# Hybrid Hyena/attention step on one core: another order of first loads and steps, modulation in four column groups, odd stream blocks by ScalarE, filters one by one between projections

## The reference, cut to what matters

```
shift, scale, gate = jnp.split(mod, 3, axis=-1)      # mod = silu(c) @ w_mod + b_mod
h = x * (1 + scale) + shift
proj = h @ p['w_in'][l]                              # 66 column blocks of 128
filt = hyena_filters(n, ...)                         # sin MLP on positions, @ w3, times a decay
y_hy = hyena(hy_in, conv_w, conv_b, filt, skip)      # 2 orders of long convolution
... differential attention, MLA, gates, merge, w_out, LayerNorm

def hyena_filters(...):
    hid = jnp.sin(sf[0] * (feats @ w1 + b1))
    hid = jnp.sin(sf[1] * (hid @ w2 + b2))
    h = hid @ w3
    h = h * jnp.exp(-t_lin[:, None] * jnp.exp(log_decay))
```

## Time and profile before

| | before |
|---|---|
| device time, median of 3 runs | 2047.17 us (2043.9 to 2050.02) |
| the profiled execution | 2044.92 us, of which the profile's span is 2043.1 us |
| PE busy | 1902.6 us, 93% of the span |
| DVE busy | 1112.3 us, 54% |
| ACT busy | 640.1 us, 31% |
| POOL busy | 495.1 us, 24% |
| granted TensorE clock, mean | 0.979 |

### The profile page before, as it was taken

The page is one execution under the profiler, slowest core; times in us unless marked ns, Lnnn a source line. Parts: engine busy times, 40 slices in busy tenths (PEclk is TensorE's granted clock), DMA queues, the critical chain, the costliest instruction groups (busy, mean ns, idle before and its releaser), DMA issues.

```text
span 2043.1 us, 28064 instructions
## 1 busy us (share of the span) xinstructions
PE 1902.6 (93%) x11444; PEld 1630.7 (80%) x11444; DVE 1112.3 (54%) x1571; ACT 640.1 (31%) x1132; POOL 495.1 (24%) x228
## 2 busy tenths in 40 slices
PE   6799899999999999999968999999999999999995
PEld 4579599887786777899965876998788777779995
DVE  3458568355343443377776775745453434444744
ACT  2231321244333444322233222123442344442221
POOL 0210104222231111276320010332222301115551
PEclk9899999999999999999978999999999999999998
DMA  9011012111220101354620111221113100114431
GB/s 343 22 36 48 31 63 73 55 45 47 78 83 21 35 32 31 109 177 139 248 83 31 42 32 31 83 68 47 42 52 109 42 23 28 32 47 132 173 109 52
DMA packets 50159, 151.83 MB, mean 74 GB/s; under 512 B 11051, under 2 KB 12587, under 8 KB 48753
## 3 DMA queue, kind: packets, MB, share of 16 engines
q1 hardware_dynamic: 46432, 135.89, 19.8%
q10 hardware_dynamic: 3600, 14.16, 2.0%
HBM read 143.43 MB, written 6.59 MB: 73 GB/s over the span
## 4 chain that ended last, share of the span: by engine, by line
PE 81%; DVE 9%; ACT 4%; issue 3%; SPq 1%; DMA 1%; POOL 1%; ACTq 0%; DVEq 0%; POOLq 0%
PE PS L776 19%; PE PS L781 18%; PE PS L777 18%; PE PS L831 6%; PE PS L967 3%; PE PS L819 2%; PE PS L1085 2%; PE PS L866 2%; PE PS L869 2%; PE PS L1018 2%; PE PS L848 2%; DVE MG L1620 1%; ACT work L1136 1%; ACT Wh L1136 1%; PE PS L1074 1%
## 5 line engine op out<-in xcount | busy, mean ns | idle before, releaser
L1780 POOL TENSOR_TENSOR Wl<-W,Wh 128x1024 fp32r<-128x1024 f32 (+1 forms) x176 | 401.2, 2282 | 1370.5 <-ACT Wh L1136 1328.4
L776 PE MATMUL PS<-Hh,Wh 128*128 128x320 f32 x2048 | 615.8, 315 | 24.6 <-DVE work L1538 10.9
L777 PE MATMUL PS<-Hl,Wh 128*128 128x320 f32 x2048 | 606.4, 311 | 0.0
L776 PEld LDWEIGHTS PS<-Hh,Wh 128*128 128x128 f32 x2048 | 387.9, 189 | 49.8 <-issue 34.7
L777 PEld LDWEIGHTS PS<-Hl,Wh 128*128 128x128 f32 x2048 | 388.0, 189 | 1.4 <-issue 1.2
L781 PE MATMUL PS<-Hh,Wl 128*128 128x320 f32 x2048 | 321.4, 309 | 0.9 <-POOL Wl L1780 0.9
L781 PEld LDWEIGHTS PS<-Hh,Wl 128*128 128x128 f32 x2048 | 305.5, 188 | 1.4 <-POOL Wl L1780 1.4
L1136 ACT ACTIVATE work<-PS 128x640 f32<-128x640 f32 (+10 forms) x322 | 180.8, 575 | 351.4 <-PE PS L831 96.8
L1400 DVE TENSOR_REDUCE st<-PS 128x1 f32<-128x640 f32 (+1 forms) x160 | 114.9, 718 | 281.1 <-PE PS L848 176.2
L1136 ACT ACTIVATE Wh<-W 128x1024 fp32r<-128x1024 f32 x196 | 185.2, 951 | 54.4 <-PE PS L781 28.7
L1248 ACT ACTIVATE th<-PS 128x640 f32<-128x640 f32 x64 | 45.1, 705 | 358.3 <-PE PS L781 358.3
(11 more groups left out here) (194 smaller groups left out, 2545.4 us busy)
## 6 DMA issues: line engine op xcount, KB each, us to landing
W<-in_w_in SPq DMA_DIRECT2D x132, 512.0 KB, 3.5
W<-in_w_branch SPq DMA_DIRECT2D x48, 256.0 KB, 2.6
work<-in_w_mod_rows ACTq DMA_DIRECT2D x23, 512.0 KB, 3.8
pmod_w<-in_w_mod SPq DMA_DIRECT2D x8, 1024.0 KB, 17.2
W<-in_w_out SPq DMA_DIRECT2D x16, 512.0 KB, 5.6
late_modulation_w<-in_w_mod_rows SPq DMA_DIRECT2D x9, 512.0 KB, 7.5
work<-in_x_sample SPq DMA_DIRECT2D x2, 2048.0 KB
x_mid<-work SPq DMA_DIRECT2D x1, 2560.0 KB, 8.4
```

The source lines that it names most:

```text
L776: pe.matmul(out, Wh[:, b, kk, :], xh[:, kk, t], start=kk == 0, stop=False)
L777: pe.matmul(out, Wh[:, b, kk, :], xl[:, kk, t], start=False, stop=False)
L1780: return pool.tensor_tensor(out, in_, high.bitcast(f32), ALU.subtract)
```

## The change

- `pmrow` has four steps in place of eight. Each takes four weight tiles; the conditioning vectors stand in a stationary operand padded with zeros to 32 columns (`cpad`), and the four tiles' results go to PSUM partitions 0, 32, 64 and 96, in the array's four column groups. One transpose of 128 x 128 follows in each of four `pmod` steps.
- First loads: constants, small tables, `feats`, `w3`, log decays, then the eight modulation tiles, weight tile 0, x, weight tile 1, the forward tables; the inverse tables and rope come at `conv` 2. The one semaphore of the Hyena tables becomes three.
- Steps of layer 0: `fdft` 0 and 1 move from ahead of `ht` 0 to after `two` 4 and `conv` 1.
- `ht` c with odd c: ScalarE does the modulation (Identity with scale and bias, from PSUM) as well as the rounding. VectorE does all eight `Hl`; GpSimd none.
- The decay buffer is given back after VectorE's second instruction of a filter (`decay_used`), not its fourth. The Exp of the log decays and the first decay of a layer move to step `lam`.
- Steps of layer 1: `filt` 0 after `two` 2, `filt` 1 after `two` 4, `filt` 2 after `two` 7, `filt` 3 ahead of `conv` 2, `filt` 4 ahead of `conv` 3. While `ht` and `two` alternate, the inner steps take two PSUM slots in turn.

```diff
+def start_steps(ahead, inside):
+    s = [("ht", c) for c in range(4)] + ahead + [("two", 0)]
+    for c in range(4, KD):
+        s += [("ht", c), ("two", c - 3)] + inside.get(c - 3, [])
+    return s + [("two", kk) for kk in range(5, KD)]
 def layer_steps(l):
     if l == 0:
-        p = [("pmod", g) for g in range(KD)]
+        p = [("pmod", g) for g in range(4)]
         f = [("ffn", 0), ("ffn", 1)] + [("filt", t) for t in range(NT)] + [("fdft", i) for i in range(5)]
-        rows = [("pmrow", g) for g in range(KD)]
-        s = [("lam", 0)] + rows[:1] + f[:1] + rows[1:3] + p[:2] + f[1:2] + rows[3:5] + p[2:4] + f[2:3]
-        s += rows[5:6] + p[4:5] + f[3:4] + rows[6:7] + p[5:6] + f[4:5] + rows[7:] + p[6:7] + f[5:6] + p[7:] + f[6:9]
-        s += START
-        s += [("conv", 0), ("conv", 1), ("fdft", 2), ("conv", 2), ("conv", 3), ("fdft", 3), ("fdft", 4)]
+        rows = [("pmrow", g) for g in range(4)]
+        s = [("lam", 0)] + f[:1] + rows[:1] + f[1:2] + rows[1:2] + p[:1] + rows[2:3] + p[1:2] + f[2:4] + rows[3:] + p[2:3]
+        s += f[4:5] + p[3:] + f[5:7] + start_steps([], {4: f[7:8]})
+        s += [("conv", 0), ("conv", 1), ("fdft", 1), ("conv", 2), ("fdft", 2), ("conv", 3), ("fdft", 3), ("fdft", 4)]
     else:
         f = [("filt", t) for t in range(NT)]
-        s = [("lam", 0)] + START
-        s += [("conv", 0), ("conv", 1)] + f[:3] + [("conv", 2)] + f[3:] + [("conv", 3)]
+        s = [("lam", 0)] + start_steps([], {2: f[:1], 4: f[1:2]})
+        s += f[2:3] + [("conv", 0), ("conv", 1)] + f[3:4] + [("conv", 2)] + f[4:] + [("conv", 3)]
         s += [("fdft", i) for i in range(5)]
...
@@ slot_table
+                if rest:
+                    s = rest[0]
+                    rest.reverse()
+                else:
+                    s = at % SLOTS
+                    at += 1
...
+            if (kind, i) == ("two", 0):
+                rest = [at % SLOTS, (at + 1) % SLOTS]
+            elif (kind, i) == ("two", KD - 1):
+                at += 2
+                rest = None
...
@@ SyncE
                 if g >= NP:
-                    sp.wait_ge(*filled(0, "pmrow", g - NP))
+                    sp.wait_ge(*filled(0, "pmrow", (g - NP) // 2))
...
-            first_modulation(0)
...
-            for part in range(4):
+            for part in range(2):
                 layer_tables(0, part)
-            for g in range(1 + len(FIRST), NP):
+            for g in range(KD):
                 first_modulation(g)
+            weight(0)
             load_x(0)
-            for g in range(NP, KD):
-                first_modulation(g)
-            sp.dma_start(rope_m[:], A["rope_m"]).then_inc(rope_here, 16)
+            weight(1)
+            layer_tables(0, 2)
...
+                    if (kind, i) == ("conv", 2) and l == 0:
+                        layer_tables(0, 3)
+                        sp.dma_start(rope_m[:], A["rope_m"]).then_inc(rope_here, 16)
...
@@ TensorE
-                pe.wait_ge(*after("h_odd" if kk % 2 else "h_even", l, kk // 2 + 1))
+                pe.wait_ge(*after("h_lo", l, kk + 1))
...
+                        for g in (2 * i, 2 * i + 1):
+                            pe.wait_ge(pmod_here[g % NP], 16 * (g // NP + 1))
+                        for k in range(KD):
+                            for j in range(4):
+                                last = pe.matmul(ps[32 * j:32 * j + 32, 0:128], cpad[:, k, :],
+                                                 pmod_w[:, (2 * i + j // 2) % NP, j % 2, k, :], start=k == 0, stop=k == KD - 1)
...
@@ ScalarE
                         act.activation(lamc[:, 4:6], lamc[:, 4:6], ACT.Exp).then_inc(sems["lam_exp"], 1)
+                        act.wait_ge(filter_here, 16 * N_FILTER * (l + 1))
+                        link(act.activation(expld, expld, ACT.Exp))
+                        act.activation(decay, expld[:, :, 0, :], ACT.Exp, scale=negt[:, 0:1]).then_inc(sems["decay_ready"], 1)
                     elif kind == "ht":
-                        act.wait_ge(*after("h_f32", l, i + 1))
+                        if i % 2:
+                            act.wait_ge(*filled(l, kind, i))
...
+                            h = th[:, 1]
+                            act.activation(h[:, 0:LAT], ps[:, 0:LAT], ACT.Identity, scale=s[:, 0:1], bias=b[:, 0:1])
+                            act.activation(h[:, LAT:NTOK], ps[:, LAT:NTOK], ACT.Identity, scale=s[:, 1:2], bias=b[:, 1:2])\
+                               .then_inc(sems["h_act"], 1)
+                            act.wait_ge(*after("h_act", l, i // 2 + 1))
+                        else:
+                            act.wait_ge(*after("h_f32", l, i // 2 + 1))
                         copy(Hh[:, i, :], th[:, i % 2]).then_inc(sems["h_hi"], 1)
...
                         if i:
-                            act.wait_ge(*after("fab_ready", l, i))
...
+                            act.wait_ge(*after("decay_used", l, i))
+                            act.activation(decay, expld[:, :, o, :], ACT.Exp, scale=negt[:, t:t + 1]).then_inc(sems["decay_ready"], 1)
@@ VectorE
+                        for c in [i - 1] * (i > 0) + [i] * (i == KD - 1):
+                            dve.wait_ge(*after("h_hi", l, c + 1))
+                            TT(Hl[:, c, :], th[:, c % 2], Hh[:, c, :].bitcast(f32), ALU.subtract).then_inc(sems["h_lo"], 1)
+                            dve.wait_ge(*own("h_lo"))
...
                         TT(oddb[:, 0], ps[:, 0:HY], decay[:, 0], ALU.mult)
-                        link(STT(oddb[:, 1], ps[:, 512:1024], hmask[:, t:t + 1], decay[:, 1], ALU.mult, ALU.mult))
+                        STT(oddb[:, 1], ps[:, 512:1024], hmask[:, t:t + 1], decay[:, 1], ALU.mult, ALU.mult)\
+                            .then_inc(sems["decay_used"], 1)
+                        dve.wait_ge(*own("decay_used"))
@@ GpSimd
-                    if kind == "ht" and i % 2 == 0:
-                        pool.wait_ge(*after("h_hi", l, i + 1))
-                        minus(Hl[:, i, :], th[:, 0], Hh[:, i, :]).then_inc(sems["h_even"], 1)
```

More of the change, by code:

```diff
@@ L225 @@
 JOBS = {
-    "pmod": lambda i: [("ss_ready", 2 * i + 2)],
+    "pmod": lambda i: [("ss_ready", 4 * i + 4)],
     "nmod": lambda i: [],
@@ L293, in slot_table @@
     for l in range(DEPTH):
+        rest = None
         for kind, i in STEPS[l]:
             for j, (name, count) in enumerate(JOBS[kind](i)):
-                late = kind == "ht" and i >= 4
-                s = (at + i % 2) % SLOTS if late else at % SLOTS
+                if rest:
[4 more added lines that the diff above has]
+                    at += 1
                 table[l, kind, i, j] = (s, uses[s], last[s])
@@ L413, in build @@
         Wh = sb("Wh", [128, 2, KD, 128], f32r)
+        Wl_at = at[0]
         Wl = sb("Wl", [128, 2, KD, 128], f32r)
+        cpad = sb("cpad", [128, KD, 32], over=Wl_at)
         MG = sb("MG", [128, KD * NTOK])
@@ L462, in area @@
                                 **{c: d for c, d in zip(names, dims)})
-        pmrow = area(work, 12816, 4, 256)[0:2]
+        pmrow = area(work, 12816, 4, 128)
         ln_gc, ln_bc = vec(vecs, "ln_g"), vec(vecs, "ln_b")
@@ L670, in layer_tables @@
                         continue
-                    if n:
-                        sp.dma_start(dst, src).then_inc(hy_here, 16)
-                    else:
-                        sp.dma_start(dst, src).then_inc(feats_here, 16)
-                    if l == 0 and n in FIRST:
-                        first_modulation(1 + FIRST.index(n))
+                    sp.dma_start(dst, src).then_inc(HERE[part], 16)
             def norm_rows(l):
@@ L878, in _ @@
                         ps = slot(l, kind, i)
-                        pe.wait_ge(pmod_here[i % NP], 16 * (i // NP + 1))
-                        for m in range(2):
-                            for k in range(KD):
-                                last = pe.matmul(ps[0:2, 128 * m:128 * m + 128], ccol[:, k, :],
-                                                 pmod_w[:, i % NP, m, k, :], start=k == 0, stop=k == KD - 1)
+                        for g in (2 * i, 2 * i + 1):
[4 more added lines that the diff above has]
+                                                 pmod_w[:, (2 * i + j // 2) % NP, j % 2, k, :], start=k == 0, stop=k == KD - 1)
                         last.then_inc(full_of(l, kind, i), 1)
@@ L888, in _ @@
                         pe.wait_ge(*after("row_ready", 0, i + 1))
-                        for m in range(2):
-                            last = transpose(ps[:, 2 * m:2 * m + 2], pmrow[:, i % 4, 128 * m:128 * m + 128], 2)
-                        last.then_inc(full_of(l, kind, i), 1)
+                        transpose(ps[:, 0:128], pmrow[:, i]).then_inc(full_of(l, kind, i), 1)
                     elif kind == "ht":
@@ L1175, in _ @@
                         act.wait_ge(*filled(l, kind, i))
-                        if i >= 4:
-                            act.wait_ge(*filled(l, "pmod", i - 4))
```

(13 more changed lines are left out.)

64 lines of the change are left out of this document (30 added, 34 removed).

## The result

| | before | after |
|---|---|---|
| median of the runs (4 each) | 2047.25 us (2043.9 to 2050.02) | 2020.54 us (2018.5 to 2021.73) |
| the profiled execution | 2044.92, span 2043.1 | 2021.73, span 2019.9 |
| granted TensorE clock, mean | 0.979 | 0.981 |

The account below looks back on a forecast made before the run. TensorE is busy 93%, so time is won only where it waits or runs at half clock, as in chains between engines at the start. 23.4 + 4.9 + 2.8 + 2.7 = 33.8 us less gives 2012 us, range 2004 to 2020.

Parts of the forecast that it names:

- the order-1 filters: Both layers: decays come 1.3 earlier, so the last filter ends 2.8 us sooner in layer 0, 2.7 in layer 1.
- `two` 0 at 53.0: Start of layer 0: the first projection starts at 53.0 us, not 83.5, 30.5 less.
- Tiles 0 and 1 "are there at 19": Loads of layer 0: the first two modulation tiles have landed at 19 us, with some 2 us of transfer lost.
- The rival of late loads: Start of layer 0: loads land late, slack 7 us for x, 3 for weight tile 1; 2016 to 2018, chance 0.11.
- "2.5 us" for every `pmrow`: Layer 0 modulation: a step of 64 matmuls takes 2.5 us, with 1.8 and 7.3 as ends.
- The two `Wl`: Start of layer 0: they follow the last decay (46.4), take 4.66 us on GpSimd and end at 52.2.
- the 0.9 for `Hl`: Start of layer 0: `Hl` 0 (0.83 on VectorE) meets the second `Wl`, so `two` 0 starts at 53.0, behind 52.2.
- Groups without overlap: Rival, `pmrow` of layer 0: column groups don't overlap, a step takes 7.3 us; 2019 us in all, chance 0.10.
- First stage slower than before: Rival, start of layer 0: no overlap and half clock, 14.6 us a `pmrow`; 2059 us in all, chance 0.03.
- VectorE isn't the bound: Rival, starts of both layers: VectorE's queue drains faster, `two` 0 starts near 50; 2005 us, chance 0.11.
- the likeliest case: Whole kernel: the forecast itself, 2012 us (2006 to 2017 by the ends of its terms), chance 0.62.

Follow-up runs that it names:

- l_tiles_first: Changed kernel with the first two modulation tiles asked for ahead of the tables and filter weights; 2015.59 us.
- r_same: The changed kernel run and profiled again, unaltered; 2020.55 us.
- y_all: Changed kernel with two modulation tiles loaded first, VectorE making `Wl` 0 and 1 of layer 0, and the decays' Exp ahead of `lam`'s; median 2010.17 us.
- w_vector: Changed kernel with `Wl` 0 and 1 of layer 0 made by VectorE, not GpSimd; 2016.82 us.
- f_decay_late: Changed kernel with the decay buffer given back after a filter's fourth instruction, as before the change; 2027.92 us.

## Why the prediction went as it did

**What held.** The change is faster, and by the mechanism named: with the long chain at the start shortened, `fdft` 0 and 1 behind it cost 7.0 (7.1 forecast), `Hh` 0 of layer 1 starts 3.1 behind the first Exp (3.4), `fdft` 0 there 48.5 and 47.3 behind the first transpose (49), the order-1 filters give 2.7 and 2.6 (2.8 and 2.7), and the collision passes to the short convolution as said. A `pmrow` takes 1.96 us at full clock, between the ends of 1.8 and 7.3; I had taken 2.5. By the 62 ns that the Trainium skill gives for the issue of a matmul when hardware decode is off (TensorE: Matmul & The Clock Gate, the section "Wait — 56ns, not 53.3ns?") it would have been an estimated 4.0. The trace shows 31 ns for each, so that floor doesn't bind here.

**What failed: `two` 0 at 53.0.** It came at 56.6 and 59.2, and four of its steps were wrong. By the means of the pairs the start of layer 0 got 24.6 us shorter, not 30.5, and that is most of the miss.

*Tiles 0 and 1 "are there at 19".* They came at 21.5. The step let the engines run full from 10.5 on; the table by stretch has 304 GB/s up to 15, which makes 2.2 MB by then, not 2.5 (0.8 us). The other 1.6 is sharing, by this sum: at 412 GB/s, 4.8 MB are in by 21.4, 0.7 more than stands up to tile 1, so tiles asked for later took a part. `l_tiles_first` shows that closing the gap, most of which the step had booked as a loss, brings 1.1 to 3.7 us at `two` 0.

*Slack for late loads.* The rival of late loads was given 7 us of slack for x and 3 for weight tile 1. The path doesn't go through x. It goes through the tiles of `pmrow` 2, since `filt` 0 stands behind that step and VectorE's chain of five filters begins there. They were forecast for 29 and came at 31.8 and at 33.0 (in `r_same`, where TensorE waited 3.9 for them). From there on nothing had slack: `filt` 0 was at 34.2 and 36.7, not 32.8, and the 2.6 between the two executions is the 2.6 between their `two` 0.

*"2.5 us" for every `pmrow`.* At full clock it is 1.96, but not every step had the full clock. In `r_same` `pmrow` 2 starts behind a wait of 3.9, and the granted clock is 0.50 while it runs. The timeline, and the table by stretch (length, busy PE with its count, PEclk, DMA share, GB/s):

```profile
32.98 3.55 PE L894 MATMUL PS<-pmod_w,cpad 128*32 128x128 f32 x64 [3.94 <-DMA pmod_w<-in_w_mod]
```

```profile
33.50:36.00 2.50, 2.50 (x55) 0.50 1.02 408
```

So 64 of these matmuls take some 3.6 us at 1.2 GHz and 1.96 at 2.4. Of the 2.6 between the two executions, 1.2 is the tiles of `pmrow` 2 and the rest this clock; in the first profile TensorE had waited only 0.52 there. The 3.64 of `pmrow` 0 is the same size. The column reads 1.00 there, as it does from 20 to 25 us in every profile but that of `y_all`. But the four matmuls of `ffn` 0, TensorE's first work in the changed kernel, take 2.47, where the kernel before has 1.34 right behind a `pmrow`; and in `y_all` `ffn` 1, which also takes 1.34 in the kernel before, takes 2.47 at a granted clock of 0.50. In all likelihood `ffn` 0 and `pmrow` 0 ran at 1.2 GHz. The prediction weighed half clock only together with groups that don't overlap.

*The two `Wl`.* The step let them collide with `Hl` 0 alone. By its own times they ran from 47.5 to 52.2 and the last filter from 46.4 to 49.2, so this collision was in the forecast's numbers and was not booked. It costs 3.8 on VectorE, 3.5 by `w_vector`; the 0.9 for `Hl` that had been booked fell away. The earlier trace rows had the price.

In sum, for the first profile: tiles, the slower `pmrow` 0 (3.64) and `ffn` 1 passed on 1.4 up to `filt` 0; the collision added 3.8; `Hl` gave back 0.9; VectorE's chain ran 0.7 tighter than forecast. 3.6, of which the collision is the largest. In `r_same` 2.6 more come from `pmrow` 2, its tiles and its clock.

**What was not in the sum: the clock in the long stages.** The forecast counted `fdft` 5 at once at full clock in layer 0, behind VectorE's last filter. The wait ahead of it grew from 0.43 to 2.57, and in the two profiles of the changed kernel the 32 instructions then took 15.70 and 15.68 (in layer 1 14.00 and 15.70):

```profile
204.68 15.70 PE L842 MATMUL PS<-work,MG 128*128 128x512 f32 x32 [2.57 <-DVE work L1564]
```

1.7 of the 2.8 won by the early decays is given back so. The dip isn't new but moved. The kernel before has 0.59 from 217.5 to 220, behind the wait in which the `Wl` held the filter, and `f_decay_late` has 0.50 from 205 to 207.5: inside the last projection, where VectorE is later anyway. In the changed kernel it is 0.50 from 205 to 207.5 as well, but that is now `fdft` 5, for which all else waits. Taking the first profiles alone, the two longest rows of the table add 4.7 and 1.1, by stretches at half clock; the repeats show that those at 550 and 615 belong to the execution and not to the change, and that the kernel before has such executions too. The Trainium skill (TensorE: Matmul & The Clock Gate, the section "What's actually happening") says that how many matmuls run at the low clock at a kernel's start differs from run to run of one kernel. These pairs of profiles show the same of stretches in its middle.

**The rivals.** Groups without overlap: excluded (1.96 against 5.96). First stage slower than before: its condition, 13 us a step, was missed by far even with the groups in turn (7.83). VectorE isn't the bound: the opposite; each microsecond added to or taken from its queue ahead of `ht` 0 showed. Loads late: happened, by 2.5 to 4 us, and its price came with no slack. The prediction held the likeliest case and this rival for alternatives, and both were half true.

**Open.** Which of several equal waits pulls the clock down in an execution; and that the clock column's 1.00 at the very start doesn't hold, which is argued from durations and not shown by a record. The parts of the change at the start of layer 0 (four steps in place of eight, the order of the loads, `fdft` 0 and 1 moved, all `Hl` by VectorE) weren't run one by one, so the 24.6 won there isn't divided among them.

## What to carry to other kernels

When a sum says when each engine runs what, lay the intervals of all engines side by side and look for pairs that are known to hold each other, in every stretch and not only at the place where the old trace had them. Slack of a load is counted to the first step that stands behind it in the order, here a filter behind the third tile pair, and not to the load that is used last. Profile both kernels twice before a difference of 2 to 5 us in a long, unchanged stage is given a cause.

## What the runs showed of the hardware

- Four column groups of 32, fp32, 128 columns: 64 matmuls in 1.96 us, 31 ns each; with the groups in turn 5.96, 93 ns each. Only the order of the instructions differs.
- The same 64 matmuls take 3.55 us where the granted clock is 0.50 (`r_same`, 33.0). At the start they take 3.64 while the column reads 1.00 (20 to 25 us above). There durations tell more than the column.
- A VectorE instruction that takes two fp32 operands from SBUF and starts inside a GpSimd `Wl` ends with it or after: 2.37, 2.82, 2.92 and 3.09 instead of 0.69 to 0.89; the two `Wl` take 5.09, with two such instructions beside them, against 4.66. One that takes an operand from PSUM isn't held: in the changed kernel's first profile 25 of the 32 instructions of L1645 (`th<-th,PS`) start inside a `Wl`, and all 32 take 0.81 to 0.82; the addition behind each, all in SBUF (L1646), takes 0.82 to 2.84. VectorE itself makes a `Wl` in 1.23.
- ScalarE's Identity with scale and bias takes 0.76 for 512 columns and 0.45 for 128, and brings no table load.
